# Hybrid streaming encoder step: x taken out of PSUM by two engines, squares after the first split of the second slot, and another order of the last transposes

## The reference

```python
for layer in range(2):
    x = x + 0.5 * swiglu(rms_norm(x, ffn1_norm[layer]), ffn1_w_in[layer], ffn1_w_out[layer])
    h = rms_norm(x, mix_norm[layer])
    x = x + (even_mixer(h) if layer == 0 else odd_mixer(h))   # attention + HGRN2 | gated DeltaNet
    x = x + 0.5 * swiglu(rms_norm(x, ffn2_norm[layer]), ffn2_w_in[layer], ffn2_w_out[layer])
y = rms_norm(x, final_norm)          # x * rsqrt(mean(x*x) + eps) * gain
# swiglu(h, w_in, w_out): gate, up = split(h @ w_in); (silu(gate) * up) @ w_out; D_FF = 2816
```

## Time and profile before

| what | value |
|---|---|
| median of 3 runs | 2489.86 us (2488.88 to 2490.13) |
| the profiled execution | 2486.5 us, span 2484.5 us |
| TensorE matmul busy | 2422.7 us (98%), 19192 instructions |
| VectorE busy | 1091.7 us (44%) |
| ScalarE busy | 795.6 us (32%) |
| GpSimd busy | 375.9 us (15%) |
| mean granted clock of TensorE | 0.995 |
| DMA | 193.66 MB, 78 GB/s on the mean |

### The profile page before, as it was taken

How to read it: one execution, slowest core, us unless ns; L and a number is a source line. 1 busy time by engine, 2 the same in 40 slices (tenths; PEclk the granted TensorE clock), 3 DMA queues, 4 the chain that set the end, 5 groups by cost and what they waited for, 6 DMA issues and landing times.

```text
span 2484.5 us, 45457 instructions
## 1 busy us (share of the span) xinstructions
PE 2422.7 (98%) x19192; PEld 2371.3 (95%) x19192; DVE 1091.7 (44%) x1422; ACT 795.6 (32%) x1022; POOL 375.9 (15%) x323
## 2 busy tenths in 40 slices
PE   7999999999989999999999999999989899999998
PEld 7999999988989999999999999999888899999998
DVE  5333323555664333322433332589455544333322
ACT  4333322233333222222222222354245543222222
POOL 2111001000231111000101100242033432011000
PEclk9999999999999999999999999999999999999999
DMA  3222223322102222222222222322200002222221
GB/s 124 97 87 86 81 93 99 102 87 65 67 27 85 86 94 91 80 81 93 85 87 98 85 78 93 84 81 85 72 10 1 10 30 99 85 85 93 89 88 55
DMA packets 191213, 193.66 MB, mean 78 GB/s; under 512 B 4811, under 2 KB 188495, under 8 KB 191082
## 3 DMA queue, kind: packets, MB, share of 16 engines
q1 hardware_dynamic: 178286, 181.64, 22.3%
q10 hardware_dynamic: 12162, 8.11, 1.1%
q0 software_dynamic: 640, 2.10, 0.3%
HBM read 185.73 MB, written 6.10 MB: 77 GB/s over the span
## 4 chain that ended last, share of the span: by engine, by line
PE 90%; DVE 6%; issue 2%; ACT 1%; POOL 0%; ACTq 0%; DMA 0%; DVEq 0%
PE ps L570 78%; PE ps L2482 2%; PE ps L2458 1%; DVE wl L555 1%; DVE cacc L1802 1%; PE ps L2590 1%; PE ps L2446 1%; PE ps L1072 0%; PE ps L2491 0%; PE ps L1540 0%; ACT cacc L1861 0%; PE ps L1688 0%; PE ps L2500 0%; PE ps L2504 0%; PE ps L2472 0%
## 5 line engine op out<-in xcount | busy, mean ns | idle before, releaser
L570 PE MATMUL ps<-xh,wh 128*128 128x272 f32 x3776 | 791.6, 291 | 3.5 <-DVE wl L555 2.8
L570 PE MATMUL ps<-xh,wl 128*128 128x272 f32 x3776 | 782.5, 289 | 0.0
L570 PE MATMUL ps<-xl,wh 128*128 128x272 f32 x3776 | 779.9, 288 | 0.0
L555 DVE TENSOR_TENSOR wl<-raw,wh 128x2048 fp32r<-128x2048 f32 (+1 forms) x173 | 390.7, 2258 | 508.4 <-ACT wh L550 508.4
L570 PEld LDWEIGHTS ps<-xh,wh 128*128 128x128 f32 x3776 | 594.2, 189 | 16.1 <-issue 9.3
L570 PEld LDWEIGHTS ps<-xl,wh 128*128 128x128 f32 x3776 | 594.6, 189 | 0.0
L570 PEld LDWEIGHTS ps<-xh,wl 128*128 128x128 f32 x3776 | 591.1, 189 | 0.0
L550 ACT ACTIVATE wh<-raw 128x2048 fp32r<-128x2048 f32 (+1 forms) x173 | 323.3, 1869 | 328.4 <-PE ps L570 323.3
L570 PE MATMUL ps<-hh,wl 128*128 128x272 f32 x1408 | 291.5, 288 | 0.0
L570 PE MATMUL ps<-hh,wh 128*128 128x272 f32 x1408 | 291.1, 288 | 0.0
L570 PE MATMUL ps<-hl,wh 128*128 128x272 f32 x1408 | 290.2, 288 | 0.0
(11 more groups left out here) (420 smaller groups left out, 2213.8 us busy)
## 6 DMA issues: line engine op xcount, KB each, us to landing
raw<-ffn_w_in SPq DMA_DIRECT2D x88, 1024.0 KB, 5.0
raw<-ffn_w_out SPq DMA_DIRECT2D x32, 1024.0 KB, 5.2
raw<-odd_w_in SPq DMA_DIRECT2D x16, 1024.0 KB, 5.6
raw<-even_w_in SPq DMA_DIRECT2D x14, 1024.0 KB, 4.9
raw<-ffn_w_out SPq DMA_DIRECT2D x16, 768.0 KB, 4.8
raw<-even_w_out SPq DMA_DIRECT2D x4, 1024.0 KB, 5.2
raw<-odd_w_out SPq DMA_DIRECT2D x4, 1024.0 KB, 5.2
xnat<-x_prompt SPq DMA_DIRECT2D x2, 1024.0 KB, 9.3
```

The source lines that it names most:

```text
L555: nc.vector.tensor_tensor(wl[slot][:, 0:kt, :], raw[slot][:, 0:kt, :], wh[slot][:, 0:kt, :].bitcast(F32), ALU.subtract).then_inc(lo_done.s ...
L570: ins = nc.tensor.matmul(ps[:, 2 * pe_out + b, 0:TH], w, r[:, rk, b * TH:(b + 1) * TH], start=first and a == 0, stop=last and a == 2)
```

## The change

At the start: TensorE's transposes of x use two pairs of banks (4 to 7) and not three, so tile m waits for the copy of tile m - 2; ScalarE copies the odd tiles of x out of PSUM and VectorE the even ones, in the order of `x_ready`; ScalarE's squares are taken out of this stretch; its first weight split comes after `xh` of tile 2, and VectorE's after `xl` of tile 3. All eight squares come in `ffn_in_act` behind the split of the second unit's weights. The first unit does both column tiles for each tile of x (`first_unit`), into banks 0 to 3.

At the end: GpSimd adds seven squares and VectorE the eighth; TensorE turns tiles 0 to 5 of the blocks 0 and 1 as soon as six `yt` are there; then the two left tiles, the ten sums, block 2, block 3 after the square roots, and block 4 after block 0 is copied. There are four pairs of banks.

```diff
@@ feed_act: the square becomes a function of its own
+        x_square(act, n, m, par)
+
+    def x_square(act, n, m, par):
         act.wait_ge(ssq_done.sem, ssq_done.at(8 * n + m - 1))
...
-    def feed_pool(pool, n):
-        for m in range(KT):
+    def feed_pool(pool, n, tiles=KT):
+        for m in range(tiles):
@@ ffn_in_pe
+                if f == 0 and isinstance(j, int) and s == 0:
+                    first_unit(u)
+                    continue
...
+        def first_unit(u):
+            for k in range(KT):
+                pe.wait_ge(xl_ready.sem, xl_ready.at(8 * n + k + 1))
+                for c in range(2):
+                    last = mm3(c, 0, k, c, xh, xl, k, k == 0, k == KT - 1)
+                    if k == KT - 1:
+                        last.then_inc((gate_psum if c == 0 else unit_done).sem, 1)
+            stats_pe(pe, n)
+            late_pe(pe)
@@ ffn_in_act, first pair, behind split_hi of unit 1
+                if f == 0:
+                    for m in range(KT):
+                        x_square(act, 0, m, m % 2)
                 stats_act(act, n)
@@ load_pe
-            if m == 2:
+            if m == 1:
                 pe.wait_ge(cols_ready.sem, cols_ready.at(1))
...
-            pe.wait_ge(x_ready.sem, x_ready.at(m - 2))
-            s = 1 + m % 3
+            pe.wait_ge(x_ready.sem, x_ready.at(m - 1))
+            s = 2 + m % 2
...
+    def take_x(eng, m):
+        eng.wait_ge(xt_done.sem, xt_done.at(m + 1))
+        eng.wait_ge(x_ready.sem, x_ready.at(m))
+
+    def load_act(act):
+        for m in range(KT):
+            s = 2 + m % 2
+            if m % 2:
+                take_x(act, m)
+                nc.scalar.activation(x[:, m, 0:SEQ], ps[:, 2 * s, :], ACT.Copy)
+                nc.scalar.activation(x[:, m, SEQ:T], ps[:, 2 * s + 1, 0:DEC], ACT.Copy).then_inc(x_ready.sem, 1)
+            act.wait_ge(x_ready.sem, x_ready.at(m + 1))
+            nc.scalar.activation(xh[:, m, :], x[:, m, :], ACT.Copy, scale=gain(0, m)).then_inc(xh_ready.sem, 1)
+            if m == 2:
+                split_hi(act, 0, 0)
@@ load_dve
-            nc.vector.tensor_copy(x[:, m, 0:SEQ], ps[:, 2 * s, :])
-            nc.vector.tensor_copy(x[:, m, SEQ:T], ps[:, 2 * s + 1, 0:DEC]).then_inc(x_ready.sem, 1)
-            if m == KT // 2:
-                split_lo(dve, 0, 0)
+            if m % 2 == 0:
+                take_x(dve, m)
+                nc.vector.tensor_copy(x[:, m, 0:SEQ], ps[:, 2 * s, :])
+                nc.vector.tensor_copy(x[:, m, SEQ:T], ps[:, 2 * s + 1, 0:DEC]).then_inc(x_ready.sem, 1)
             if m:
...
                 feed_dve(dve, 0, m - 1)
+            if m == KT // 2:
+                split_lo(dve, 0, 0)
@@ output_pe
+        pe.wait_ge(y_scaled.sem, y_scaled.at(KT - 2))
+        for b, r in YB[0:2]:
+            for m in range(KT - 2):
+                nc.tensor.transpose(ps[0:r, 2 * b + m // 4, (m % 4) * P:(m % 4 + 1) * P], yt[:, m, b * P:b * P + r], ident[:])
         pe.wait_ge(y_scaled.sem, y_scaled.at(KT))
-        for b, r in YB[0:3]:
-            rows(b, r)
+        for b, r in YB[0:2]:
+            rows(b, r, KT - 2)
         pe.wait_ge(ssq_done.sem, ssq_done.at(8 * (n + 1)))
...
         ins.then_inc(ssq_psum.sem, 1)
+        rows(*YB[2])
+        pe.wait_ge(rms_ready.sem, rms_ready.at(n + 1))
+        rows(*YB[3])
         pe.wait_ge(y_act.sem, y_act.at(1))
-        rows(*YB[3])
-        pe.wait_ge(y_dve.sem, y_dve.at(1))
         rows(*YB[4])
@@ output_dve
+        dve.wait_ge(sq_ready.sem, sq_ready.at(8 * (n + 1)))
+        dve.wait_ge(ssq_done.sem, ssq_done.at(8 * n + KT - 1))
+        nc.vector.tensor_tensor(ssq[:], ssq[:], sq[1][:], ALU.add).then_inc(ssq_done.sem, 1)
```

More of the change, by code:

```diff
@@ L653, in pair @@
                             last.then_inc((gate_psum if s == 0 else up_psum).sem, 1)
-                    if isinstance(j, int) and s == 0 and c == (1 if f == 0 else 0):
+                    if isinstance(j, int) and s == 0 and c == 0:
                         stats_pe(pe, n)
-                        if f == 0:
-                            late_pe(pe)
                 last.then_inc(unit_done.sem, 1)
+        def first_unit(u):
[7 more added lines that the diff above has]
+            late_pe(pe)
         pair(0)
@@ L2653, in load_dve @@
         for m in range(KT):
-            dve.wait_ge(xt_done.sem, xt_done.at(m + 1))
-            s = 1 + m % 3
-            nc.vector.tensor_copy(x[:, m, 0:SEQ], ps[:, 2 * s, :])
-            nc.vector.tensor_copy(x[:, m, SEQ:T], ps[:, 2 * s + 1, 0:DEC]).then_inc(x_ready.sem, 1)
-            if m == KT // 2:
-                split_lo(dve, 0, 0)
+            s = 2 + m % 2
+            if m % 2 == 0:
+                take_x(dve, m)
+                nc.vector.tensor_copy(x[:, m, 0:SEQ], ps[:, 2 * s, :])
+                nc.vector.tensor_copy(x[:, m, SEQ:T], ps[:, 2 * s + 1, 0:DEC]).then_inc(x_ready.sem, 1)
             if m:
@@ L2689, in y_banks, with rows @@
     def y_banks(b, r):
-        return ps[0:r, 2 * (b % 3):2 * (b % 3) + 2, :]
+        return ps[0:r, 2 * (b % 4):2 * (b % 4) + 2, :]
     def output_pe(pe, n):
-        def rows(b, r):
-            for m in range(KT):
-                ins = nc.tensor.transpose(ps[0:r, 2 * (b % 3) + m // 4, (m % 4) * P:(m % 4 + 1) * P],
+        def rows(b, r, m0=0):
+            for m in range(m0, KT):
+                ins = nc.tensor.transpose(ps[0:r, 2 * (b % 4) + m // 4, (m % 4) * P:(m % 4 + 1) * P],
                                           yt[:, m, b * P:b * P + r], ident[:])
             ins.then_inc(y_psum.sem, 1)
+        pe.wait_ge(y_scaled.sem, y_scaled.at(KT - 2))
+        for b, r in YB[0:2]:
+            for m in range(KT - 2):
+                nc.tensor.transpose(ps[0:r, 2 * b + m // 4, (m % 4) * P:(m % 4 + 1) * P], yt[:, m, b * P:b * P + r], ident[:])
         pe.wait_ge(y_scaled.sem, y_scaled.at(KT))
-        for b, r in YB[0:3]:
-            rows(b, r)
+        for b, r in YB[0:2]:
+            rows(b, r, KT - 2)
         pe.wait_ge(ssq_done.sem, ssq_done.at(8 * (n + 1)))
@@ L2776, in _ @@
         act.wait_ge(cols_ready.sem, cols_ready.at(1))
[L2777 to L2780, removed]
+        load_act(act)
         ffn_in_act(act, 0, 0)
@@ L2810, in _ @@
         ffn_in_pool(pool, 3, 5)
-        feed_pool(pool, 6)
+        feed_pool(pool, 6, KT - 1)
     @block.vector
```

## The result

The changed kernel takes 2492.70 us (median of 20 runs, 2491.03 to 2493.71), the kernel before 2489.03 us (20 runs, 2485.45 to 2490.25): ratio 1.0016, 95% interval 1.0010 to 1.0022, so 3.7 us slower, between 2.5 and 5.5. The forecast was +6.4 us. The time lies in the forecast range (2491.5 to 2499.5), but outside the part that was the forecast's own (2494.5 to 2498.5), and the difference of 0.15% is under the 0.2% above which I had expected it with a chance of 0.66.

The account below looks back on a forecast made before the run. TensorE's matmuls bound the kernel, so only its waits in the first 43 and last 15 us counted. Terms +4.3 (wait), +4.0 (slow clock) and -1.9 (end) made +6.4 on 2489.86, 2496.3 us; range 2491.5 to 2499.5.

Parts of the forecast that it names:

- the part that was the forecast's own: Main forecast without the rivals: about 2496.3 us, own range 2494.5 to 2498.5, chance 0.57.
- First unit at 23.05 without a stop, gone by 37.1: Start: TensorE's first matmuls begin at 23.05 against 22.97, run without the 0.9 us stop and end 0.9 earlier.
- rival (c): Start: ScalarE's four copies take 1.4 each, not 0.84; everything from the squares on slips up to 2 us; 2498.5; chance 0.17.
- Sum ready at 42.3, +4.3: Start: GpSimd's sum of squares is ready at 42.3, so the statistics matmuls start there and not at 38.02, +4.3 us.
- The standstill: Start: GpSimd's first copy of a square waits until VectorE's second weight split ends, stretched to about 2.2 us.
- Rival (b): Start: sum of squares ready before the first unit ends; TensorE wins 0.9 there and 1.9 at the end; 2487.1; chance 0.06.
- Slow clock, +4.0: After TensorE's 5.2 us wait, clock at 0.50: statistics +0.8, transposes and what follows +1.5, second unit +1.7; between 0 and +5.0.
- Rival (a): Start: the wait is there, but the clock costs next to nothing; +4.3 - 1.9 + 0.5, 2492.8 us; chance 0.20.
- The end, -1.9: End: square roots and first outputs 1.8 earlier, last output issued 2.4 earlier, output DMAs limiting the gain; -1.8 to -2.4.
- The sum: Whole kernel: +4.3 for the wait, +4.0 for the clock, -1.9 for the end, together +6.4 us.

Follow-up runs that it names:

- all seven profiles of the table: Start cost read at the first addition of a product to x: four profiles with the old start, mean 325.07; three with the changed start, 331.86.
- end-only kernel: The kernel before with the changed end alone (six tiles turned ahead, four bank pairs, last square added by VectorE): 2486.29 us, ratio 0.9993.

## Why the prediction was right in its mechanism and too large in its sum

- **First unit at 23.05 without a stop, gone by 37.1**: it began at 22.22 and ended at 35.6. 0.4 of that is the gains' DMA (8.31 against 8.70). ScalarE's copy of a tile took 0.67 (13.47 to 14.14), not 0.84 and less than the bound of 0.7, and the chain of copies ran ahead of the forecast by about 0.4 more. The last 0.7 is the unit itself, 13.4 us and not 14.1: its matmuls are 0.23 apart until 24.7, 2.4 us, where the first profile of the kernel before has 4.2 us of that rate and the sum took over 4. (The granted clock reads 1.00 in both stretches.) No harm came from the copies: rival (c) is out.
- **Sum ready at 42.3, +4.3**: it was ready at 41.0, the statistics came 3.0 later than in the earlier trace rows and not 4.3, 3.4 without the DMA's luck. The standstill was right (2.10 against "about 2.2"); the rest is the earlier front and additions of 1.33 to 1.36. Rival (b) is out: the sum came 5.4 after the unit's end.
- **Slow clock, +4.0**: between the two profiles it is +1.1 for the statistics, +1.85 for the constants and 3.5 x 0.42 = +1.5 for the second unit, 4.4. As a cost of the changed kernel the step was right. The statistics took twice their time and not 1.7 times. Rival (a), the clock for next to nothing, names the measured time (2492.8), but by a step that the trace refutes; that the range held 2492.70 is owed to having taken in that rival.
- **The end, -1.9**: -2.2 between the profiles, -2.0 measured alone, with an interval that holds no gain. The last output was issued 2.4 sooner and the span ended 2.2 sooner, so the DMAs took back 0.2 of it and not 0.5.
- **The sum**: 3.0 + 4.4 - 2.2 = 5.2 between the profiles; they differ by 5.3 in span. The forecast was 6.4. So 1.2 of its excess of 2.7 is the terms: 1.3 too much for the sum of squares and 0.3 too little for the end, against 0.4 too little for the clock.
- **From the profiles to the medians**: the other 1.5 lies between 5.2 and the 3.7 of the medians, and the interval of 2.5 to 5.5 is wide enough to hold it. It touches the second paragraph's "I work out a difference in the profiled execution and put it on the median", which took the slow clock as +4.0 over a kernel that has none. The kernel before has some of it in three of the four profiles with its start, 3.4 to 6.8 us, which in the second unit and the constants comes to 1.4 to 3.0. Taken over all seven profiles of the table the start cost 6.8 and not 7.5, and 6.8 - 2.2 = 4.6. The rest of the way to 3.7 has no cause that a run shows: the three profiled executions of the kernel before lie 1.3 to 2.5 under the medians of their groups, also those with slow clock, and the changed kernel's two 1.1 under its own. I noted the 3.4 between the profiled execution and the median before the prediction and did not ask what could make it; it is still open.

## What to carry to other kernels

Moving work off the stretch in which it is in the way is worth nothing if it comes back as a chain that the bottleneck engine waits for: count the chain at its slowest link (eight tiles at 1.54 us) against the time that covers it, and give it to the engine that is idle there (VectorE did the same sums at 0.83 a tile). When the profiled execution lies at the edge of the spread of runs, take more profiles of the same kernel before adding a difference to the median, and compare them at one instruction behind the stretch in question. And TensorE's small transposes are better placed where nothing has to wait for them: moving them off the wait for the square root came out 2.8 us faster, at an interval that reaches from nothing to 4.5.

## What the runs showed of the hardware

The granted clock fell to 0.50 after stretches in which TensorE was hardly idle: it did behind statistics, 1.0 us of wait and 29 transposes of at most 7 columns in the end-only kernel (6.8 us of 1.2 GHz) and in the second and third profile of the kernel before (3.4 us), and did not in the first. It also fell, for 3.4 us, in both profiles of the kernel with VectorE's sums and the constants in the second unit, with no idle time of TensorE between 35 and 44 us. GpSimd's copy beside a VectorE subtraction of two SBUF tiles took 2.10 us against 0.68. ScalarE reads 512 columns from PSUM in 0.58 us where VectorE takes 0.68.
